# Expert jobs with token rows fetched through DRAM, a 0/1 scatter of y split in halves, eleven weight slots and four pairs of split weights

## The reference, cut to what matters

```python
logits = einsum('btd,de->bte', h, router)          # 8 experts
top_v, top_i = top_k(logits, 2); probs = softmax(top_v)
for e in range(8):
    y = y + gates[..., e] * ((silu(h @ wg[e]) * (h @ wu[e])) @ wd[e])   # width 2816
```

## Time and profile before

| | |
|---|---|
| median of 3 runs | 1745.01 us (1737.62 to 1747.04) |
| the profiled execution | 1745.35 us, its span 1743.4 us |
| mean granted TensorE clock | 0.965 of full speed |
| busy share of the span | TensorE 94%, VectorE 71%, ScalarE 54%, GpSimd 1% |
| moved by DMA | 386 MB, of it 277 MB of expert weights |

### The profile page before, as it was taken

One profiled execution on the slowest core, in us unless ns is written; L12 is line 12 of the kernel. 1 busy time (PEld: TensorE's weight loads), 2 busy tenths in 40 slices (PEclk: granted clock), 3 DMA queues, 4 the chain that ended last, 5 costly groups with the idle time before them and its releaser, 6 DMA issues.

```text
span 1743.4 us, 31379 instructions
## 1 busy us (share of the span) xinstructions
PE 1645.7 (94%) x11185; PEld 1479.8 (85%) x11185; DVE 1239.8 (71%) x1797; ACT 945.2 (54%) x1297; POOL 12.6 (1%) x27
## 2 busy tenths in 40 slices
PE   5998999899998898999889999999999999999996
PEld 4978887899986888887879798998979889798995
DVE  3776855544203687855379899898988989899896
ACT  4632151444202642151258687786877778687784
POOL 0000000000000000000000000000000000000000
PEclk9989899899999999899889999999999999999999
DMA  6441124455444551124249899797988979899793
GB/s 256 147 109 55 49 79 165 161 182 182 144 145 156 164 126 61 49 69 148 104 171 362 299 351 368 284 358 291 357 339 313 364 286 357 302 348 367 284 364 145
DMA packets 103844, 386.14 MB, mean 221 GB/s; under 512 B 11697, under 2 KB 11729, under 8 KB 103009
## 3 DMA queue, kind: packets, MB, share of 16 engines
q1 hardware_dynamic: 102096, 372.00, 60.6%
q0 software_dynamic: 1680, 13.20, 2.2%
HBM read 377.79 MB, written 7.37 MB: 221 GB/s over the span
## 4 chain that ended last, share of the span: by engine, by line
PE 85%; DVE 8%; ACT 3%; issue 2%; DMA 1%; SPq 0%; DVEq 0%; POOL 0%; ACTq 0%
PE psum L1205 57%; PE psum L1451 5%; PE psum L1238 3%; PE psum L1485 3%; PE psum L1416 2%; PE psum L1543 2%; PE psum L1418 2%; DVE w_lo L736 1%; PE psum L1311 1%; PE psum L1318 1%; PE psum L1375 1%; DVE qkv L806 1%; PE psum L1322 1%; ACT w_hi L471 1%; DVE c L837 1%
## 5 line engine op out<-in xcount | busy, mean ns | idle before, releaser
L1140 DVE TENSOR_TENSOR w_lo<-ring,w_hi 128x1024 fp32r<-128x1024 f32 x528 | 644.5, 1224 | 73.3 <-ACT w_hi L693 66.4
L693 ACT ACTIVATE w_hi<-ring 128x1024 fp32r<-128x1024 f32 x528 | 557.9, 1061 | 142.9 <-PE psum L1205 135.2
L1205 PE MATMUL psum<-w_hi,h_hi 128*96 128x256 f32 x1408 | 402.2, 286 | 5.5 <-DVE w_lo L1140 5.5
L1205 PE MATMUL psum<-w_hi,h_lo 128*96 128x256 f32 x1408 | 394.9, 280 | 0.0
L1205 PE MATMUL psum<-w_lo,h_hi 128*96 128x256 f32 x1408 | 393.6, 280 | 0.0
L1205 PE MATMUL psum<-hid_hi,w_hi 128*128 128x264 f32 x992 | 293.2, 296 | 17.8 <-issue 9.2
L1205 PE MATMUL psum<-hid_lo,w_hi 128*128 128x264 f32 x992 | 287.5, 290 | 0.0
L1205 PE MATMUL psum<-hid_hi,w_lo 128*128 128x264 f32 x992 | 287.1, 289 | 0.0
L736 DVE TENSOR_TENSOR w_lo<-ring,w_hi 128x1024 fp32r<-128x1024 f32 x124 | 150.5, 1220 | 127.7 <-ACT w_hi L471 127.4
L1205 PEld LDWEIGHTS psum<-w_hi,h_hi 128*96 128x96 f32 x1408 | 228.6, 162 | 8.7 <-DVE w_lo L1140 7.4
L471 ACT ACTIVATE w_hi<-ring 128x1024 fp32r<-128x1024 f32 x124 | 131.0, 1059 | 182.3 <-PE psum L1205 140.8
(11 more groups left out here) (292 smaller groups left out, 1759.3 us busy)
## 6 DMA issues: line engine op xcount, KB each, us to landing
ring<-in_w_exp SPq DMA_DIRECT2D x528, 512.0 KB, 5.2
ring<-in_w_mixer SPq DMA_DIRECT2D x112, 512.0 KB, 3.5
ring<-in_w_ffn SPq DMA_DIRECT2D x66, 512.0 KB, 3.5
early<-in_s POOLq DMA_DIRECT2D x2, 2048.0 KB, 7.9
out_ss<-early POOLq DMA_DIRECT2D x2, 2048.0 KB, 9.0
xT<-in_xT SPq DMA_DIRECT2D x1, 1056.0 KB, 5.0
out_yT<-hT POOLq DMA_DIRECT2D x1, 1056.0 KB, 4.2
u_win<-in_dw_win POOLq DMA_DIRECT2D x2, 496.0 KB, 5.5
```

The costliest lines, as they stand in the source:

```text
L693: A(w_hi[:, (n_split + u) % SPLIT, :], ring[:, u % RING, :, :].rearrange("p k n -> p (k n)"), ACT.Copy).then_inc(hi_done, 1)
L1140: V.tensor_tensor(w_lo[:, (n_split + u) % SPLIT, :], ring[:, u % RING, :, :].rearrange("p k n -> p (k n)"), w_hi[:, (n_split + u) % SPLIT, ...
L1205: last = M(out, lhs[x], rhs[w], start=(start and n == 0), stop=(stop and n == 2))
```

## The change

- SPLIT goes from 3 to 4. A new constant LEAD = 3 takes its place where the queues say how many units ahead of its use a unit is split, so the order of the mixers' queues is unchanged.
- Experts: 11 weight slots instead of 6; the five new ones lie in `early` (four) and `qkv`, which layer 1 has done with by then. Their first load waits until the last states are written out.
- Experts: tokens go through DRAM. In layer 0, after the merge, POOL clears `h_rows` (1440 rows of 4 KB, twelve transfers) and `meta_rows`. After the router POOL writes each token's row of h to its place with six indirect transfers (three tiles of tokens, two choices), and (gate, token number) to `meta_rows` with six more. Job 0 is still gathered by TensorE, in both halves before the loop. For each later job SP loads 96 rows in one transfer (384 KB) and 96 x 2 values, after 44 of the job's 66 weight units. TensorE turns them with 8 transposes after unit 52 (`turn_rows`); ScalarE and VectorE split them after unit 53.
- y of a job is scaled by its gate and split: ScalarE writes `y_hi` (`y_high`), VectorE `y_lo` and a 0/1 matrix of tokens (`y_low`). The halves lie in pair 3, which is kept for them between units 2 and 3 of the next job. The scatter has two matmuls a tile, in halves of four tiles before units 3 and 5; VectorE's adds follow after units 4 and 6. After the loop stands one more y, scatter and adds, for the last job. Job 0 scatters zeros.
- Gone: the broadcast of slots and gates over rows before the loop, `take` for later jobs, `put`, `y_tok`, both gathers inside the loop, and the wait of the first gate/up units for the adds (the first transposes wait for them now).

```diff
-SPLIT = 3
+SPLIT = 4
+LEAD = 3
+NEXT_H = 52
+RING_X = 11
+Y_AT = 3
...
-                for i in range(2, 2 + SPLIT):
+                for i in range(2, 2 + LEAD):
                     high_part(section, i)
...
+        def buffer_x(u):
+            v = u if u < Y_AT else u + 1
+            return v % SPLIT if v < N_FFN + 1 - SPLIT + 1 else v - (N_FFN + 1 - SPLIT + 1)
...
+            def load_rows(job):
+                sp.wait_ge(gather_mm, job * 2 + 2)
+                sp.dma_start(h_row, h_rows[bass.ds(job * CAP + CAP, CAP), :]).then_inc(row_loaded, 16)
+                sp.wait_ge(y_lo_done, job + 1)
+                sp.dma_start(meta_job[0:CAP, :], meta_rows[bass.ds(job * CAP, CAP), :]).then_inc(meta_loaded, 16)
+            late = N_FFN // RING_X * 2 // 3
+            load_units(0, 0, 1, late)
+            sp.wait_ge(rows_stored, 16 * 12)
+            load_rows(0)
+            load_units(0, 0, late, N_FFN // RING_X)
...
+            for i in range(6):
+                pool.indirect_dma_start(h_rows, bass.IndirectOffsetOnAxis(ap=row_at[:, i:i + 1], axis=0), h_tok[:, i % 3, :], None,
+                                        bounds_check=JOB_ROWS - 1, oob_is_err=False).then_inc(rows_stored, 16)
...
+                            if u == Y_AT:
+                                y_high(job)
+                            act.wait_ge(slot_loaded[u % RING_X], job * (16 * N_FFN // RING_X) + 16 * (n0[u % RING_X] + u // RING_X + 1))
+                            if buffer_x(u) == Y_AT % SPLIT and u < Y_AT + SPLIT:
+                                act.wait_ge(scatter_mm, job * KD + KD)
+                            else:
+                                act.wait_ge(units_used, job * N_FFN + (base_ord["experts"] + used_before_x(u) + 1))
+                            A(w_hi[:, buffer_x(u), :], slot_x(u % RING_X), ACT.Copy).then_inc(hi_done, 1)
+                            if u == NEXT_H + 1:
+                                gathered(job + 1, 0)
+                                gathered(job + 1, 1)
...
+                            V.tensor_tensor(w_lo[:, buffer_x(u), :], slot_x(u % RING_X), w_hi[:, buffer_x(u), :], ALU.subtract).then_inc(lo_done, 1)
+                            if u == Y_AT - 1:
+                                y_low(job)
+                            if u == Y_AT + 1:
+                                add_rows(job, 0)
+                            if u == Y_AT + 3:
+                                add_rows(job, 4)
+                            if u == NEXT_H + 1:
+                                h_low(job + 1, 0)
+                                h_low(job + 1, 1)
...
+                    def scatter(job, t0):
+                        pe.wait_ge(y_lo_done, job + 1)
+                        for t in range(t0, t0 + 4):
+                            if t >= 4:
+                                pe.wait_ge(down_taken, job * KD + (KD + t - 3))
+                            M(psum[:, 4 + t % 4, 0:T], y_hi[:, t * P:(t + 1) * P], pick_token, start=True, stop=False)
+                            M(psum[:, 4 + t % 4, 0:T], y_lo[:, t * P:(t + 1) * P], pick_token, start=False, stop=True).then_inc(scatter_mm, 1)
...
-                        gather(job, 1)
                         for u in range(N_FFN):
                             if u < 2:
                                 pe.wait_ge(h_job_done, job * 2 + (u + 1))
+                            if u == Y_AT:
+                                scatter(job, 0)
+                            if u == Y_AT + 2:
+                                scatter(job, 4)
...
+                            if u == NEXT_H:
+                                turn_rows(job)
```

More of the change, by code:

```diff
@@ L403, in _ @@
                 expert = sp.value_load(jobs[0:1, bass.ds(job, 1)], min_val=0, max_val=NE - 1)
-                load_expert(expert, job, 0)
+                load_units(expert, job, 0, late)
+                load_rows(job)
+                load_units(expert, job, late, N_FFN // RING_X)
         @block.gpsimd
@@ L586, in z_silu @@
                     A(zs[:, t, :], psum[:, (Z_AT + t) % 4, 0:T], ACT.Silu).then_inc(act_evac, 1)
-                    high_part(section, Z_AT + t + SPLIT)
+                    high_part(section, Z_AT + t + LEAD)
                 def gates(n0, n1):
@@ L707, in _ @@
                                 A(act_hi[:, 2 * ch:2 * ch + 2, :].rearrange("p f s -> p (f s)"), psum[:, 4 + ch % 2, 0:2 * CAP], ACT.Copy).then_inc(act_hi_done, 1)
[L709 to L713, removed]
+                    act.wait_ge(meta_loaded, n_jobs * 16)
+                    y_high(n_jobs)
+                    act.wait_ge(down_taken, n_jobs * KD + 2 * KD)
             model_squares(2 * DEPTH)
@@ L1115, in _ @@
                     V.tensor_copy(jobs[:, 0:MAX_JOBS], scan[:, 0:2, :].rearrange("p a b -> p (a b)")[:, 0:MAX_JOBS]).then_inc(jobs_done, 1)
[L1117 to L1127, removed]
+                    V.tensor_copy(meta[:, :, 0], gates)
+                    for i in range(6):
+                        ins = V.tensor_scalar(meta[:, i, 1:2], par("slot_col", 0), float((0, P, T - P)[i % 3]), None, ALU.add)
+                    ins.then_inc(row_at_done, 1)
+                    for i in range(0, T, CAP):
+                        V.tensor_scalar(token_row[:, i:min(i + CAP, T)], par("slot_row", 0, min(CAP, T - i)), float(i), None, ALU.add)
+                    V.memset(meta_job[:, 0:1], 0.0)
+                    V.memset(meta_job[:, 1:2], -1.0).then_inc(meta_clear, 1)
                     dve.wait_ge(jobs_done, 1)
@@ L1535, in _ @@
                                 last.then_inc(act_tr, 1)
-                        gather(job + 1, 0)
-                        pe.wait_ge(y_tok_done, job + 1)
-                        pe.wait_ge(put_done, job + 1)
-                        for t in range(KD):
-                            if t >= 4:
-                                pe.wait_ge(down_taken, job * KD + (KD + t - 3))
-                            M(psum[:, 2 + t % 4, 0:T], y_tok[:, t * P:(t + 1) * P], put, start=True, stop=True).then_inc(scatter_mm, 1)
-                    pe.wait_ge(down_taken, n_jobs * KD + KD)
+                            if u == NEXT_H:
+                                turn_rows(job)
+                    scatter(n_jobs, 0)
+                    scatter(n_jobs, 4)
+                    pe.wait_ge(down_taken, n_jobs * KD + 2 * KD)
             model_sums(2 * DEPTH)
```

171 lines of the change are left out of this document (102 added, 69 removed).

## The result

The changed kernel takes **1715.13 us** (median of 4 runs, 1711.22 to 1718.77), against 1741.42 for four runs of the kernel before on the same chip: a ratio of 0.9846, interval 0.9804 to 0.9888. It is faster by 1.5%. The forecast was faster too, but 1728; the measured time lies at the very low end of the range. Executions of one kernel differ by several us (those of the kernel before ran at 1736.02 to 1748.06 us in all, at mean granted clocks of 0.974 to 0.963), so a few us between two medians tell nothing. The profiled execution took 1717.27 us, its span is 1715.5 us, 27.9 less than the span of before.

A forecast was written before the change was run, and what follows sets the result against it. TensorE, busy 94% of the span, was taken to bound the kernel, with VectorE close behind in the jobs. 1745.3 - 13.5 (mixers) - 3.7 (experts) gave 1728 us, range 1715 to 1748.

The forecast's parts named there:

- Part 1, the mixers: Heads of both mixers: a fourth pair removes the 4.6 us waits and slow units behind them, 13.5 us gained.
- Part 2, a job: One expert job: 103.2 us instead of 104.7, bounds 102.2 to 105.5; with the tail, 3.7 us gained over the experts.
- TensorE's own work: Expert job: chunks, down units, scatter and transposes take 97.1 us if nothing waits, plus 0.2 added from the kernel before.
- The three waits: Expert job: new TensorE waits of 2.1 us before unit 54, 1.2 at unit 6 and 1.6 at unit 7.
- I take a fall in something over half of the jobs, +1.0: Expert job: half speed for 3.2 us loses 1.6 per clock fall, counted as 1.0 us a job.
- The wait before unit 54: Expert job: copies and splits of the fetched rows chain for about 3.5 us, unit 53 covers 1.39, 2.1 us lost.
- the rule taken from the earlier trace: TensorE's clock: 1.8 us idle was followed by a fall to 0.50, 1.3 us idle left it at 1.00.
- the clock holds in the jobs: Rival for the expert jobs: all waits too short for a fall, 102.2 us a job, 1720 us in all; chance 0.23.
- The tail: Behind the expert loop: a last y copy, split, scatter and eight adds, 6.1 us in all.
- Part 3, at nothing: Weight transfers, row load, clearing h_rows, job 0's indirect transfers and the start of the experts: all costed at 0.
- VectorE's burst: Rival behind the job boundary: VectorE's queue becomes the bound, 107 us a job, 1758 us in all; chance 0.09.
- The fourth pair: Rival in the mixers: another wait of the same length stands behind the one removed, nothing freed, 1741 us; chance 0.10.

The follow-up runs named there:

- the two runs on the pair: Kernel before with a fourth pair in mixers and feed-forward block only: 1726.8 us; changed kernel with those splits waiting for the third unit back: 1731.42 us.
- the jobs without waits: Changed kernel with fetched-row splits after unit 55, y's halves in own rows, adds spread two at a time: 1682.84 us; also last y in halves: 1682.11 us.
- five copies: Changed kernel with five idle ScalarE copies behind the splits of the fetched rows, lengthening the wait before unit 54: median 1743.91 us.
- the three copies: Changed kernel with three idle ScalarE copies ahead of the splits of the fetched rows: 1713.39 us.

## Why the prediction was right in sign and wrong in size

**Part 1, the mixers: right mechanism, a little short.** Exponentials at 32, no wait, no slow units behind it: as forecast, and the two runs on the pair show that it is the cause. The sum of 13.5 us measured 16, inside its bounds (0 to 17). The rest is the clock later in the mixer. In layer 1 of the profiled executions 10.5 us were gained, 4.58 of them the wait; the other 5.9 are clock, by the mean granted clock of the stretches: 0.06 x 305 - 0.04 x 294.5 = 6.5, of which I had counted 2.4. Where the clock falls later in a mixer differs between executions of the same work: in the profiled executions that share the changed mixers, layer 0's mixer ended anywhere from 309.4 to 315.8 us. In the changed kernel, at 315.7, the low clock that begins near 195 us lasts 20.5 us; in the one with y's own rows, at 309.4, it lasts 10.2. So it is not settled whether those later falls go with the wait.

**Part 2, a job: this is where it failed.** 103.2 us was forecast, 101.47 measured. TensorE's own work with its small stops is 97.7, as the jobs without waits show (forecast 97.1 + 0.2). The three waits cost the other 3.8, of which the list counts 1.44 + 0.99 + 1.16 = 3.6 (forecast 2.1 + 1.2 + 1.6 = 4.9). The clock costs 0 (forecast 1.0). So two steps failed, of about equal size: the lengths of the three waits, 1.1 too long, and "I take a fall in something over half of the jobs, +1.0". TensorE's own work was put 0.4 too low.

The wait before unit 54 was over-sized most, 2.1 against 1.44. My chain began at the end of the turn and was 3.5 us long. In the trace the turn is told to ScalarE in halves: the chain leaves it after four of the eight transposes, at 956.93 above, 0.3 us before its end, and reaches unit 54 at 960.08, 3.15 us later.

The clock was the error of principle: the rule taken from the earlier trace rows, that 1.8 us idle lets the clock fall and 1.3 us doesn't. In the jobs 2.4 us never did, and 3.0 us did in three jobs of eight. So before unit 54 even a wait as long as forecast would not have brought the fall; longer waits at units 6 and 7 were not tried. In the mixer, where the row was read, the clock also falls with no wait over 0.9 us, so the row did not show that its wait brought the fall. What does bring it stays open. Its price was right: 1.6 us forecast, 1.6 measured with five copies.

The rival "the clock holds in the jobs" gave 1720 us and came nearest. The Trainium skill, "TensorE: Matmul & The Clock Gate", section "Why this matters for your kernels", which warns only of longer gaps, forecast that the clock holds. The trace agrees in the jobs (1.44 us and 2.4 us, 1.00 behind them) and not outside them: 1.8 us in the mixer of before and 2.5 us in the tail are followed by 0.50. The page's rule was the better guide here, mine had one row behind it. A job of 101.47 us lies below this rival's 102.2 too, so its clock was right and its waits were too long.

**The tail: its clock was not costed.** The last y was put at 6.1 us (the terms written beside it add up to 5.85) and took 1694.2 - 1687.3 = 6.9, and the final norm behind it 2.3 more than before. That the wait of 2.5 us would let the clock fall over both was not foreseen, though that wait was in the sum and longer than those for which I did price a fall.

So the experts gave 15.2 instead of 3.7: 8 x 1.73 = 13.8 from the jobs, less 0.8 in the tail and 1.5 for a slower first job. Of that 1.5, 1.4 is clock: behind the wait of 5.2 us at the start, TensorE runs at 0.50 from 874.0 to 876.8, which was not in the sum. That 1715 lies so near the forecast is partly luck: the jobs gave more than forecast, and the tail, the start of the first job and the end took some of it back.

**Part 3, at nothing: right within 2 us.** The further slots give some 2 us in the traces and nothing that the medians can tell. Clearing h_rows is free: the kernel with the fourth pair alone, which clears nothing, ends its dense block at 537.1 us, the changed one at 537.0. The start of the experts is 0.5 us later. One loss was in no part of the sum: the 2.1 us behind the issue of the last output transfer, whose cause is open.

**The other rivals.** VectorE's burst did not become the bound: with all waits away the same work fits into 97.7 us a job. The fourth pair did free the mixers.

## What to carry to other kernels

Price a wait by its length first, and put a clock fall behind it only when the trace shows one at a wait of the same length amid the same work, and even then as a chance (three of eight at 3.0 us). Before a row is taken for a rule, look whether the same stretch shows the effect without the supposed cause. Where three waits of 1 to 1.5 us stand in a loop that runs eight times, look which queue holds the late instruction: moving the splits by two units, giving y rows of its own and spreading eight adds took all of it back, 3.8 us a job. Work added to a queue ahead of a wait that ends later anyway costs nothing, as the three copies showed.

## What the runs showed of the hardware that was not expected

The granted clock answers to a wait of TensorE in no single way. Between stretches of dense matmuls in a job, 1.76 us and 2.4 us were never followed by the 1.2 GHz level in the profiled executions, 3.0 us in three jobs of eight. In the mixer of before 1.8 us was followed by it, and so was 2.5 us behind the last job in nine of ten profiled executions. In the mixer of the changed kernel the clock fell where no wait was over 0.9 us. The kernel with a wait of 3.0 us in each job of its profiled execution ran at 1731 or at 1744 us; whether the slower executions had more falls, no trace shows.
